# A hybrid encoder kernel: the first layer's preparation, attention and recurrence joined in one part of the program, with the order of three engines written anew

## The reference

```python
p = rms_norm(x, norm1) @ w_in            # 20 tiles of 128 columns
y_a = rwkv7_mixer(p[..., :RW_IN], ...)   # 8 heads of 64, forward and backward
y_b = gqa_axial_attention(p[..., RW_IN:], q_norm, k_norm)   # 8 query heads, 2 key heads
x = x + concatenate([y_a, y_b], -1) @ w_out
x = x + swiglu(rms_norm(x, norm2), ffn_gate, ffn_up, ffn_down)
```

```python
sa  = einsum('bhvk,bhk->bhv', state, a_t)          # a_t = -kk
new = state * w_t + sa * b_t + v_t * k_t           # b_t = kk * a
out = einsum('bhvk,bhk->bhv', new or state, r_t)
```

## Time and profile before

| | us |
|---|---|
| median of 3 runs | 1643.25 (1642.49 to 1643.83) |
| the profiled execution's own time | 1644.72 |
| its span, first to last instruction | 1642.9 |
| PE busy, share of the span | 1569.9 (96%) |
| DVE busy | 1259.3 (77%) |
| ACT busy | 1055.2 (64%) |

### The profile page before, as it was taken

The page is one execution under the profiler, slowest core; times in us unless marked ns, Lnnn a source line. Parts: engine busy times, 40 slices in busy tenths (PEclk is TensorE's granted clock), DMA queues, the critical chain, the costliest instruction groups (busy, mean ns, idle before and its releaser), DMA issues.

```text
span 1642.9 us, 29979 instructions
## 1 busy us (share of the span) xinstructions
PE 1569.9 (96%) x11044; PEld 1234.9 (75%) x11044; DVE 1259.3 (77%) x1524; ACT 1055.2 (64%) x1425; POOL 0.2 (0%) x4
## 2 busy tenths in 40 slices
PE   7987888999999899999999999999999999999997
PEld 6866787999999878777777777777776777777774
DVE  6855436656555875789889899889889989889886
ACT  5663344444445435777777777777777777778774
POOL 0000000000000000000000000000000000000000
PEclk9988999999999999999999999999999999999999
DMA  8002004444544313699999999999999999999993
GB/s 338 11 1 117 4 4 155 181 171 184 191 156 154 116 42 118 244 379 359 365 371 369 355 369 368 361 365 371 361 368 368 353 372 373 353 368 363 368 369 119
DMA packets 100923, 425.42 MB, mean 259 GB/s; under 512 B 8160, under 2 KB 8160, under 8 KB 95344
## 3 DMA queue, kind: packets, MB, share of 16 engines
q1 hardware_dynamic: 100848, 424.38, 68.8%
HBM read 423.30 MB, written 1.05 MB: 258 GB/s over the span
## 4 chain that ended last, share of the span: by engine, by line
PE 61%; DVE 1%; ACT 0%; issue 0%; DVEq 0%
PE bank L158 19%; PE bank L156 19%; PE bank L157 19%; PE bank L1866 1%; PE bank L1886 1%; PE bank L1816 1%; DVE w_low L153 0%; PE bank L2141 0%; PE bank L1839 0%; ACT xn L2168 0%; DVE x_tok_low L2032 0%; ACT scratch L2170 0%; DVE xn L2119 0%; DVE bank L2107 0%; PE bank L1805 0%
## 5 line engine op out<-in xcount | busy, mean ns | idle before, releaser
L153 DVE TENSOR_TENSOR w_low<-ring,w_high 128x1024 fp32r<-128x1024 f32 x801 | 932.1, 1217 | 45.6 <-ACT w_high L150 45.5
L150 ACT ACTIVATE w_high<-ring 128x1024 fp32r<-128x1024 f32 x801 | 799.9, 1049 | 73.7 <-PE bank L158 53.9
L156 PE MATMUL bank<-w_high,slots_high 128*96 128x512 f32 x448 | 179.6, 401 | 0.0
L156 PE MATMUL bank<-w_high,more_slots_high 128*96 128x512 f32 x448 | 179.6, 401 | 0.0
L156 PE MATMUL bank<-w_high,turned_high 128*96 128x512 f32 x448 | 175.0, 391 | 2.3 <-DVE turned_low L153 2.1
L158 PE MATMUL bank<-w_high,more_slots_low 128*96 128x512 f32 x448 | 176.8, 395 | 0.0
L158 PE MATMUL bank<-w_high,slots_low 128*96 128x512 f32 x448 | 176.8, 395 | 0.0
L158 PE MATMUL bank<-w_high,turned_low 128*96 128x512 f32 x448 | 176.6, 394 | 0.0
L157 PE MATMUL bank<-w_low,turned_high 128*96 128x512 f32 x448 | 175.9, 393 | 0.0
L157 PE MATMUL bank<-w_low,slots_high 128*96 128x512 f32 x448 | 175.4, 391 | 0.0
L157 PE MATMUL bank<-w_low,more_slots_high 128*96 128x512 f32 x448 | 175.3, 391 | 0.0
(11 more groups left out here) (346 smaller groups left out, 2424.2 us busy)
## 6 DMA issues: line engine op xcount, KB each, us to landing
ring<-in_w_moe SPq DMA_DIRECT2D x224, 1024.0 KB, 6.5
ring<-in_w_moe SPq DMA_DIRECT2D x224, 512.0 KB, 6.1
ring<-in_w_ffn SPq DMA_DIRECT2D x22, 1536.0 KB, 6.6
ring<-in_w_in SPq DMA_DIRECT2D x15, 1536.0 KB, 6.8
ring<-in_w_out SPq DMA_DIRECT2D x6, 1536.0 KB, 7.5
scratch<-in_x SPq DMA_DIRECT2D x2, 512.0 KB, 4.2
out_y<-xn SPq DMA_DIRECT2D x4, 256.0 KB, 2.9
const<-in_const SPq DMA_DIRECT2D x1, 948.0 KB, 13.2
```

What stands on the lines that cost most here:

```text
L150: return nc.scalar.activation(dst, src, ACT.Copy)
L153: return nc.vector.tensor_tensor(dst, src, high.bitcast(f32), sub)
L156: nc.tensor.matmul(out, left[0], right[0], start=start, stop=False, **flags)
```

## The change

The code of the first block moves into four functions, `prepare_loads`, `prepare_products`, `prepare_activations` and `prepare_elementwise`, which each engine runs at the head of the second block. There is no block end between attention and recurrence. In its place stand single waits: a new semaphore `factors_ready` (8 counts, one for each finished factor in the order B[0], A[0], B[1], R[1], A[1], R[0], K[0], K[1]), and waits on `pair_taken`, `gate_copied`, `tile_shifted`, `heads_copied` for the banks.

The order of all three engines is written out anew. `rope` moves from the scratch area of A into a ring slot and `run[1]` into the place of v, so that A is free before the attention begins. The exponentials of the decays move ahead of, or into, the first attention units. On PE `scores(0)` and `scores(1)` come one projection earlier. The bonus leaves the preparation: its head sums stand within `recur(1)`, its product with v on DVE before the state of step 1, and the rest of the bonus and gate work between the levels of the second pair of steps.

```diff
-        rope, v_rows, stats = area(A_, 5, S), area(A_ + 1280, S), area(TEMP_ + 3840, 3, 16)
+        v_rows, stats = area(A_ + 1280, S), area(TEMP_ + 3840, 3, 16)
-        run = [slot_area(3, 2048, RT, S), area(A_ + 1536, RT, S)]
+        run = [slot_area(3, 2048, RT, S), area(V_, RT, S)]
+        rope, rope_flat = slot_area(0, 1024, 5, S), slot_area(0, 1024, 5 * S)
...
+            project(11)
+            pe.wait_ge(rope_ready, 1)
+            scores(0)
+            scores(1)
+            project(12)
+            project(13)
+            pe.wait_ge(v_tok_ready, 1)
+            turn(0)
+            scores(2)
+            turn(1)
+            scores(3)
+            project(14)
+            weigh(0)
+            project(15)
+            weigh(1)
+            turn(2)
+            scores(4)
+            project(16)
+            weigh(2)
+            turn(3)
+            scores(5)
+            project(17)
+            key_sums()
+            weigh(3)
+            turn(4)
+            scores(6)
+            project(18)
+            weigh(4)
+            turn(5)
+            scores(7)
+            project(19)
+            weigh(5)
+            turn(6)
+            gate_up_product()
+            weigh(6)
+            turn(7)
+            weigh(7)
...
+            take_moving(4)
+            split_high(act, 5, TILES_DONE[3])
+            act.wait_ge(run_ready, 2)
+            nc.scalar.activation(flat(sig[:, 1]), flat(sig[:, 1]), ACT.Exp, scale=-DECAY_C).then_inc(scales_ready, 1)
+            nc.scalar.activation(flat(A[:, 1]), flat(run[1]), ACT.Exp, scale=DECAY_C).then_inc(scales_ready, 1)
+            take_moving(5)
+            nc.scalar.activation(factor, factor, ACT.Exp, scale=-DECAY_C).then_inc(scales_ready, 1)
+            act.wait_ge(rope_ready, 1)
+            act_then(act, nc.scalar.activation(flat(R[:, 0]), flat(run[0]), ACT.Exp, scale=-DECAY_C))
+            nc.scalar.activation(flat(run[0]), flat(run[0]), ACT.Exp, scale=DECAY_C).then_inc(scales_ready, 1)
+            exponentials(0)
+            exponentials(1)
+            keys_mixed(0)
+            take_moving(6)
+            copy_turned(0)
+            nc.scalar.activation(flat(A[:, 0]), flat(sig[:, 0]), ACT.Exp, scale=-DECAY_C).then_inc(scales_ready, 1)
+            exponentials(2)
+            copy_turned(1)
+            exponentials(3)
+            split_high(act, 6, TILES_DONE[4])
+            key_squares()
+            copy_turned(2)
+            copy_heads(0)
+            exponentials(4)
+            take_moving(7)
+            keys_mixed(1)
+            copy_turned(3)
+            exponentials(5)
+            key_norm()
+            copy_turned(4)
+            copy_heads(1)
+            exponentials(6)
+            take_moving(8)
+            copy_turned(5)
+            exponentials(7)
+            copy_turned(6)
+            copy_heads(2)
+            take_moving(9)
+            copy_turned(7)
+            act.wait_ge(gate_done, 1)
+            act.wait_ge(summed, 7)
+            for n in range(2):
+                nc.scalar.activation(halves(gate, n), two(2 + n), ACT.Copy).then_inc(gate_copied, 1)
+            copy_heads(3)
...
+            split_low(dve, 5)
+            maximum(0)
+            maximum(1)
+            shift(1)
+            normalise(0)
+            normalise(1)
+            shift(2)
+            shift(3)
+            maximum(2)
+            normalise(2)
+            maximum(3)
+            normalise(3)
+            keys(0)
+            split_low(dve, 6)
+            maximum(4)
+            normalise(4)
+            maximum(5)
+            shift(4)
+            key_floor()
+            normalise(5)
+            keys(1)
+            maximum(6)
+            dve.wait_ge(kk_scale_ready, 1)
+            dve_then(dve, nc.vector.tensor_tensor(flat(kk), flat(kk), flat(kk_scale), mul))
+            dve_then(dve, times(B[:, 0], rate[:, 0], kk))
+            normalise(6)
+            dve.wait_ge(scales_ready, 4)
+            nc.vector.tensor_tensor(flat(B[:, 0]), flat(B[:, 0]), flat(run[0]), mul).then_inc(factors_ready, 1)
+            dve_then(dve, times(B[:, 1], rate[:, 1], kk))
+            maximum(7)
+            dve.wait_ge(scales_ready, 5)
+            minus_kk(0)
+            normalise(7)
+            nc.vector.tensor_tensor(flat(B[:, 1]), flat(B[:, 1]), flat(sig[:, 1]), mul).then_inc(factors_ready, 1)
+            shift(5)
+            shifts_done(6)
+            nc.vector.tensor_tensor(flat(R[:, 1]), flat(A[:, 1]), flat(r_in), mul).then_inc(factors_ready, 1)
+            dve.wait_ge(factors_ready, 4)
+            minus_kk(1)
+            shift(6)
+            nc.vector.tensor_tensor(flat(R[:, 0]), flat(R[:, 0]), flat(r_in), mul).then_inc(factors_ready, 1)
+            for i in range(RT):
+                nc.vector.scalar_tensor_tensor(bonus[:, i], r_in[:, i], par("r_k", i), K[:, 0, i], mul, mul).then_inc(bonus_in, 1)
+            dve.wait_ge(bonus_in, 4)
+            for d, scale in ((0, run[0]), (1, sig[:, 1])):
+                nc.vector.tensor_tensor(flat(K[:, d]), flat(K[:, d]), flat(scale), mul).then_inc(factors_ready, 1)
...
+                prepare_loads(sp)
+                sp.wait_ge(factors_ready, 8)
+                sp.wait_ge(heads_copied, 4)
...
+                    if s == 0:
+                        pe.wait_ge(factors_ready, 5)
...
+                        if s == 0 and bank == 1:
+                            pe.wait_ge(factors_ready, 6)
+                            pe.wait_ge(pair_taken, 7)
+                        if s == 0 and bank == 3:
+                            pe.wait_ge(factors_ready, 8)
...
+                            if s == 0 and bank + d in (2, 3):
+                                pe.wait_ge(gate_copied, bank + d - 1)
...
+                    if s == 1:
+                        bonus_sums(0)
...
+                    if s == 1:
+                        bonus_sums(1)
...
+                        if s and n in (1, 2):
+                            for i in (2 * n - 2, 2 * n - 1):
+                                last = nc.vector.scalar_tensor_tensor(bonus[:, i], bonus[:, i], par("gn_b", i), gate[:, i], add, mul)
+                            dve_then(dve, last)
+                        if s and n == 3:
+                            nc.vector.memset(v_tok[:, :, :], 0.0)
+                            for i in range(RT):
+                                last = nc.vector.tensor_scalar(gate[:, i], gate[:, i], par("gn_w", i), None, mul)
+                            dve_then(dve, last)
...
+                        if r == 1:
+                            for n in range(2):
+                                dve.wait_ge(bonus_sum, n + 1)
+                                dve_then(dve, nc.vector.tensor_tensor(halves(bonus, n), two(4 + n), halves(v_in, n), mul))
```

More of the change, by code:

```diff
@@ L380, in program @@
          keys_ready, kk_sq_ready, kk_sum_ready, kk_floor_ready, kk_scale_ready, gate_done, gate_copied, run_ready,
-         scales_ready, bonus_in, bonus_sum) = (sem(n) for n in names)
+         scales_ready, bonus_in, bonus_sum, factors_ready) = (sem(n) for n in names)
         PAIR_OF = [0, 1, 2, 3, 0, 1, 2, 1, 2, 1]
@@ new lines, in prepare_loads @@
+        def prepare_loads(sp):
+            for t in range(TT):
+                sp.dma_start(x_tok[:, t], io["x"][t * P:(t + 1) * P, :]).then_inc(x_loaded, 16)
+            first = CONST["cos"][0]
+            sp.dma_start(const[:, 0:first], io["const"][:, 0:first]).then_inc(consts_loaded, 16)
+            sp.dma_start(param[:, :], io["param"]).then_inc(consts_loaded, 16)
+            for g in range(N_IN0):
+                load_group(sp, g, stream[g])
+                if g == 1:
+                    sp.dma_start(const[:, first:], io["const"][:, first:]).then_inc(rest_loaded, 16)
+                    sp.dma_start(small[:, :], io["small"]).then_inc(rest_loaded, 16)
@@ L950, in _ @@
             def _(pe):
+                prepare_products(pe)
                 def chunk(v, s, d, t, h):
@@ L986, in grams @@
                         wait_for_bank(0, n + 2)
+                        if s == 0 and n == 2:
+                            pe.wait_ge(tile_shifted, 7)
+                            pe.wait_ge(heads_copied, 4)
                         for d, t, h in SYSTEMS:
@@ L1021, in levels, with bonus_sums @@
                             level(n, q)
+                def bonus_sums(n):
+                    pe.wait_ge(bonus_in, 4)
+                    nc.tensor.matmul(ps[4 + n][:, :], cst("headsum"), halves(bonus, n), start=True, stop=True).then_inc(bonus_sum, 1)
                 def recur(s):
@@ L1379, in _ @@
                         y_out(r)
-                        if r == 0:
-                            for i in range(RT):
-                                last = nc.vector.scalar_tensor_tensor(bonus[:, i], bonus[:, i], par("gn_b", i), gate[:, i], add, mul)
-                            dve_then(dve, last)
-                        if r == 1:
-                            nc.vector.memset(v_tok[:, :, :], 0.0)
```

(3 more changed lines are left out.)

689 lines of the change are left out of this document (287 added, 402 removed).

## The result

The changed kernel takes 1623.88 us, the median of 4 runs (1622.32 to 1629.35), beside 1643.54 (1642.49 to 1643.99) before: ratio 0.9884, 95% interval 0.987 to 0.9897. The forecast was 1623.2, range 1619.5 to 1630.0. Measured again twice beside the experiments it took 1622.68 (0.9872, 0.9851 to 0.9893) and 1624.44 (0.9883, 0.9867 to 0.99), so it is 1622.7 to 1624.4 from one set of runs to the next.

The account below looks back on a forecast made before the run. No engine was full; a chain of waits between engines bound attention and preparation. Grams 20.7 us earlier less 0.6 for the bonus sums gave 20.1 off 1644.72, 1624.6, and 1.47 lower as median: 1623.2, range 1619.5 to 1630.

Parts of the forecast that it names:

- The chain: Preparation, from the rotary embedding to the second gram: steps summed across engines put `grams(1)` at 133.1, 20.7 us earlier.
- The clock behind the grams: K's grams and the start of the next: low TensorE clock after PE's idle pieces, taken as 0.8 us.
- The bound of 2.1: Most the low clock could cost at the grams: 0.9 + 1.2 = 2.1 us, the difference of the two grams.
- The clock in attention: Sign of a wrong prediction: granted clock between 70 and 120 us not 1.00.
- The table load: ACT, before the key norm's exponential: load of 1.28 us without the skill page's drain, which would give 1624.6.
- The bonus in `recur(1)`: Two head sums of 0.99 us each where PE waits 0.70: 0.6 us added, at least 0, at most 2.0.
- The sum: Whole kernel: 20.7 - 0.6 = 20.1 us off the profiled execution's 1644.72 gives 1624.6, as median 1623.2.
- Rival A: Preparation chain: a late unit keeps the 4.7 us hole before a turn, plus 2.1 of clock; 1630.0; chance 0.20.
- B's low clock in the recurrence: From the grams' start: clock stays low through levels and recurrence, costing 24 us; 1647; chance 0.03.
- C's fixed start of the feed-forward: Feed-forward start: something else, say a load, fixes it and the gain is given back; 1643; chance 0.02.
- D's: Whole kernel: clock stays up and added sums hide, 1643.25 - 21.5 - 0.5 = 1621; chance 0.74 together with the forecast.

Follow-up runs that it names:

- the execution at 1623.80: The changed kernel profiled a third time, nothing altered; that execution's own time is 1623.80 us, the median of its set of runs 1624.44 us.
- the filled kernel: Changed kernel plus idle PE products in its holes: 2 before `turn(1)`, 3 before B's grams, 4 before K's; 1624.48 us, ratio 0.9888.
- the last swap: `copy_turned(0)` ahead of `take_moving(6)` on ACT, atop the changed kernel with `keys(1)`, K[1] x sig[1] and `rate x run` made early on DVE; 1620.41 us.

## Why the prediction was right

Times from the rotary embedding's end, the prediction's beside those of the execution at 1623.80:

| step | predicted | measured |
|---|---|---|
| `turn(0)` starts, no wait | 7.5 | 7.4 |
| `turn(1)` waits for `copy_turned(0)` | 0.9 | 0.90 |
| key sums end | 32.2 | 31.9 |
| DVE waits for the key norm | 0.8 | 0.80 |
| first gram | 50.5 | 50.6 |
| B's products | 53.7 | 53.2 |
| K's products | 57.8 | 57.2 |
| second gram | 63.2 | 63.4 |

**The chain.** Each step held within 0.6 us. It could be summed from the rows of before, since all durations stood there and only the starts had to be worked out. One part of the gain the prediction had in its sum without naming it. It took each step at its full-clock duration (3.06 for a tile, 0.6 for a turn), so closing the waits of `turn(u)` also took back the low clock behind them. That is most of the 6.8 us estimated above: before, the low clock cost 8.6 us by the same count (64.6 - 56.0), and only 2.1 of them in the grams. PE is the bound up to the first gram; from the key norm to K[1] it is DVE, as written. The moves of the first scores, the exponentials and the bonus, each undone alone, cost 4.1, 2.5 and 3.6 us of distance. With the joined block's 3.5 that is 13.7 of 20.4, if they simply add up, which no run tests. The other changes of order weren't undone one by one.

**The clock behind the grams.** Mis-sized: 0.8 us was the term, 1.6 the measured cost, as the transposes fall under the low level too. The total didn't show it because B's and K's factors came half a microsecond earlier than summed: that the second gram is only 0.2 off is partly luck. The bound of 2.1 held and wasn't reached.

**The clock in attention.** "It is wrong if ... the granted clock between 70 and 120 isn't 1.00": that came in one of three executions, behind a hole of 0.90 that I had forecast but given no clock term. It costs 1.5 us of distance. Had it been the rule, the forecast would be 1.5 too low. Five of the experiments have the same single hole of 0.9 to 1.0 before `turn(1)`, and all five show 1.00 from 80 to 90, so it is one profile of eight. Behind the grams' holes of 1.5 and 2.0 the low level came each time, in five profiles of five. The page "TensorE: Matmul & The Clock Gate" of the Trainium skill, Part 1, has the throttled state as the default and activity as what releases it, and the runs side with it so far: with idle products in the holes the clock stayed at 1.00 behind them. What decides between the two levels behind one and the same hole, no run here shows.

**The table load.** The logarithm ends at 107.95, the load of 1.28 us starts at 107.97, and the exponential at 109.27 follows it at once, as in the rows of before. So the row was the right choice over the drain that the Trainium skill gives ("ScalarE: Activation LUTs", "What ACT_TABLE_LOAD costs"): no 1380 ns stand before the load or behind it.

**The bonus in `recur(1)`.** +0.6 us forecast. DVE's rows for this step before (L1375 is its first, L1377 the last) and after (L1442 and L1444; L1436 the products with v):

```profile
187.82 0.69 DVE L1375 TENSOR_TENSOR ring<-bank,cols 128x512 f32<-128x512 f32 x1 [6.78 <-PE bank L1044]
...
196.28 0.69 DVE L1377 TENSOR_TENSOR ring<-bank,ring 128x512 f32<-128x512 f32 x1 [4.26 <-PE bank L1044]
```

```profile
171.18 0.69 DVE L1442 TENSOR_TENSOR ring<-bank,cols 128x512 f32<-128x512 f32 x1 [7.19 <-PE bank L1095]
...
175.97 0.69 DVE L1436 TENSOR_TENSOR scratch<-bank,scratch 128x512 f32<-128x512 f32 x1 [2.17 <-PE bank L1068]
...
180.23 0.69 DVE L1444 TENSOR_TENSOR ring<-bank,ring 128x512 f32<-128x512 f32 x1 [1.37 <-PE bank L1095]
```

From the first to the last it is 8.46 us before and 9.05 after: +0.6. DVE waits for PE all along, so its products with v hide. The stretch behind the second gram, 97.3 before, is 97.1, 94.9 and 96.5 in the three executions.

**The sum.** 20.4 us of distance and -0.6 make 19.8; the medians differ by 19.7, 20.8 and 19.7. The forecast was 20.1. That the agreement is this close is luck in part: the stretch behind the second gram alone differs by 2.2 us between executions of the changed kernel. From the last output's product to the end of the span it is 1391.8 us before and 1392.4 to 1393.5 after, so nothing was given back there beyond a microsecond or so. Rival A's extra stretch of waits, B's low clock in the recurrence (1.00 from 145 to 230) and C's fixed start of the feed-forward did not come. Two sums of the rivals are loose: B's is 1643 - 20 + 24 = 1647, not 1627 + 20, and D's takes off 0.5 us that no term of it gives.

## What to carry to other kernels

Where no engine is full, sum the chain from durations in the trace, engine by engine, and name at each point who is late next; here each step held to within 0.6 us. Take full-clock durations only if the sum also closes the holes: of this gain about a third was the clock. After such a change ask anew what is the bound: the next 4 us lay in work on DVE that could be done before the late operand came. Where TensorE is the bound, price a hole with the work behind it at the low clock too: beyond their own length, the pair of 1.03 and 0.90 cost 2.9 us, the grams' 1.5 and 2.0 cost 1.6, and the single 0.90 cost 1.5 in one profile and nothing in seven.

## What was not expected of the hardware

**One hole, two clocks.** Behind the same 0.90 us hole the granted clock from 80 to 90 was 0.84 and 0.81 in one execution and 1.00 in two of the same program (and in five of programs with the same order there); two holes of 1.03 and 0.90 in 2.6 us gave 0.62 and 0.70. What decides it is open.

**Idle time that nothing explains.** Between the second gram and the last output's product PE idles in small pieces at the head of levels, which the profile puts down to no one:

```profile
PE bank L1051 <- issue: 2.9, 5, 0.9
PE bank L1048 <- issue: 2.9, 4, 0.7
```

This is the first execution of the changed kernel, 5.8 us. In the second it is 3.7, in the third 4.7, before it was 6.2, in the other kernels 4.3 to 6.4. The stretch less this idle time is 91.1 us before and 90.7 to 92.4 in all twelve other profiles, while the stretch itself runs from 94.9 to 98.2. So more than half of the differences in the recurrence go with it, and it can hide gains below some 2 us; that it did so with the filled kernel and the last swap is argued, not shown. Its cause wasn't found. The start of the kernel adds to this: over the changed kernels the rotary embedding ends anywhere from 68.24 to 72.10.
